# A two-layer streaming encoder step: query and key loads of the prompt attentions as 128-row transfers from one two-plane tensor

## The chip, the cores and the metric

One Trainium2 chip, one core of it. A core has five engines with their own instruction queues: TensorE (matmul; PE in the profile, its weight loads PEld), VectorE (DVE), ScalarE (ACT), GpSimd (POOL) and SyncE (SP), which here issues all the transfers; the transfers run on 16 DMA engines. Engines wait for each other by semaphores. The metric is the device time of one execution, in microseconds (us), as the median of several runs. TensorE's clock has two levels, 1.2 and 2.4 GHz; the profile gives the granted clock as a share of 2.4 GHz.

## The reference

The program is one step of a two-layer encoder, all in float32, on 1,024 frames of a new stream (the prompt) and on 16 new frames of each of 8 running streams (the samples), whose past is cached. Layer 0 has two attentions side by side: A, a sliding-window attention with 8 query and 2 key/value heads and a learned sink in each softmax, and B, a differential attention with 4 heads, each of two softmaxes. Layer 1 has C, a forgetting attention with 16 heads. A feed-forward block follows each. Cut to what matters here:

```python
# A (prompt): block-causal band of 3 chunks of 64 frames, 8 heads of 64
scores = q @ k.T * SCALE;  p = softmax([scores, sink])[..., :-1];  out = p @ v
# B (prompt and samples): 8 query/key halves of 64, 4 value heads of 128
p = softmax(where(chunk_mask, q2 @ k2.T * SCALE, NEG));  out = (p[0] - lam * p[1]) @ v
# C (prompt and samples): 16 heads of 64, c = cumsum(log_sigmoid(f)) along the frames
scores = q @ k.T * SCALE + c[query] - c[key];  p = softmax(where(causal, scores, NEG));  out = p @ v
```

## The kernel before, in words

The program runs in stages with a barrier of all engines between them: a projection of layer 0 (named abp in the profile), the prompt's window attention (pa), the samples' window attention (sa), a joint stage for the prompt's and the samples' differential attention (jb), output projection and feed-forward (abm, f), projection of layer 1 (c), the joint stage of the forgetting attention (jc), and again output projection and feed-forward (cm, f).

Queries and keys are kept in two parts. A float32 value is split into a high part that a fast matmul takes exactly and a low part, the rest. The projections write, for each of the prompt's queries (scaled) and keys, a row of 1,024 frames (4,096 bytes) into a tensor of high parts (`hi_ab`, `hi_c`) and one of low parts (`lo_ab`, `lo_c`) in the chip's memory. One head has 64 such rows. The scores of a query tile of 128 frames (`score`, L964 for pa and L1481 for jb and jc) are two matmuls for each piece of up to 512 keys, added up, and one that adds the mask:

- `q_hi` against `k_both`: `k_both` holds the key's 64 high rows on partitions 0 to 63 and its 64 low rows on 64 to 127; `q_hi` holds the query's high rows twice, so that the 128 products are high times high plus high times low.
- `q_lo` against `k_both` (pa, jb): the query's low rows twice. In jc instead `q_lo` against `k_hi` with 66 rows: 64 low rows against 64 high rows, and two rows of ones, which GpSimd writes once into `q_lo` (L1451 to L1454), against two rows of forget sums (`ck`).

So a head is loaded with six transfers of 64 rows (256 KB each), or with seven in jc (the seventh are the two rows of `ck`), by `load_qk` (L879 in pa, L1307 in jb and jc). The buffers hold two heads; a transfer group has one semaphore for each of the two, and the first `score` of a head waits for all of its transfers (L968, L1487); in pa it waits for the values and the sink of the head too (L969).

All transfers go out on SP's queue in the order written there. In pa: queries and keys, values, and sink of head 0, the same of head 1, and then for each head that is done the next but one. In jb and jc (L1381 to L1396): queries and keys of head 0, values, the key cache of the first sample stream (four transfers of 1 MB), the sample queries (four transfers with pieces of 256 bytes), then a wait for GpSimd's setup, small tables, the samples' new keys, queries and keys of head 1, its values. After that a loop over the units `u` (a head of the prompt and a stream of the samples each) issues the loads of the next units (L1397 to L1414).

TensorE works through an order that is written out by hand: for step `n` of a head `score(n+3)`, `turn(n+1)` (transposes of the probabilities), parts of the sample work, `attend` (probabilities times values). In the unit's step 5 it calls `score_new` (L1578 to L1581), which needs query blocks that VectorE copies (L1813) after it has turned the samples' new keys (L1828); `attend` (L1522) needs VectorE's scaling of the output before (L1803 or L1799). VectorE takes the maxima (L1768), turns the key cache 32x32-wise (L1822), and does the small sums.

Of the kernel before, what the change touches and what calls it, by code (L numbers as in the profile page):

```python
# [18 lines left out]
F32 = mybir.dt.float32  # L19
# [6 lines left out]
P = 128  # L26
D = 1024
# [757 lines left out]
def prompt_attention(nc, name, trips, q_rows, k_rows, v_cols, o_cols, hi, lo, y, o, dv, window=False,  # L785
# [40 lines left out]
    with Stage(nc, name) as st:  # L826
# [26 lines left out]
        n_qk_loads = 6 if ck is None else 7  # L853
# [20 lines left out]
        @block.sync  # L874
        def _(sp):
            if diff:
                sp.dma_start(lam[:], rows(b_lambda.rearrange("(a n) d -> a (n d)", a=1))).then_inc(lam_loaded, 16)

            def load_qk(i, e):  # L879
                k, q = bass.ds(k_rows(i, e), DH), bass.ds(q_rows(i, e), DH)  # L880
                upper, lower = slice(0, DH), slice(DH, P)
                sp.dma_start(k_both[upper, e].bitcast(F32), hi[k]).then_inc(qk_loaded[e], 16)
                sp.dma_start(q_hi[upper, e].bitcast(F32), hi[q]).then_inc(qk_loaded[e], 16)
                sp.dma_start(k_both[lower, e].bitcast(F32), lo[k]).then_inc(qk_loaded[e], 16)
                sp.dma_start(q_hi[lower, e].bitcast(F32), hi[q]).then_inc(qk_loaded[e], 16)
                sp.dma_start(q_lo[upper, e].bitcast(F32), lo[q]).then_inc(qk_loaded[e], 16)
                if ck is None:
                    sp.dma_start(q_lo[lower, e].bitcast(F32), lo[q]).then_inc(qk_loaded[e], 16)
                else:
                    sp.dma_start(k_hi[upper, e].bitcast(F32), hi[k]).then_inc(qk_loaded[e], 16)  # L890
                    sp.dma_start(k_hi[DH:DH + 2, e].bitcast(F32), ck[bass.ds(2 * i + e, 1)].rearrange(
                        "h a n -> (h a) n")).then_inc(qk_loaded[e], 16)

            def load(i, e):
                sp.dma_start(v[:, e], y[0:PROMPT, bass.ds(v_cols(i, e), dv)].rearrange(
                    "(t p) d -> p t d", p=P)).then_inc(loaded[e], 16)
                if sinks is not None:
                    s_i = sinks[0:1, bass.ds(2 * i + e, 1)]
                    sp.dma_start(sink[:, e:e + 1], rows(s_i)).then_inc(loaded[e], 16)

            def store(i, e):
                if diff and e == 0:
                    return
                sp.wait_ge(out_done, 2 + units * i + TILES_P * (e + 1))
                sp.dma_start(o[0:PROMPT, bass.ds(o_cols(i, e), dv)].rearrange("(t p) d -> p t d", p=P),
                             out[:, e]).then_inc(stored[e], 16)

            for q in stored:
                sp.nop().then_inc(q, 16)
            load_qk(0, 0)  # L910
            load(0, 0)
            load_qk(0, 1)
            load(0, 1)
            for i in range(trips - 1):
                for e in range(2):
                    sp.wait_ge(scores_done, units * i + TILES_P * (e + 1))
                    load_qk(i + 1, e)
                    sp.wait_ge(pv_done, 4 + units * i + TILES_P * (e + 1))
                    load(i + 1, e)
                    store(i, e)  # L920
            for e in range(2):
                store(trips - 1, e)
            sp.wait_ge(stored[1], 16 * (trips + 1))
            if not diff:
                sp.wait_ge(stored[0], 16 * (trips + 1))
# [223 lines left out]

def strided(ap, offset, *dims):  # L1150

    return bass.AP(ap.tensor, ap.offset + offset, [list(ap.ap[0])] + [list(d) for d in dims])


def joint_attention(nc, name, groups, hi, lo, k_first, v, v_cols, dv, q_sample, q_first, k_cache, v_cache, k_new, v_new,
# [79 lines left out]
    with Stage(nc, name) as st:  # L1235
        q_rows_lo = P if ck is None else DH + 2
        q_hi, k_both = st.sb("q_hi", [P, 2, PROMPT], F32R), st.sb("k_both", [P, 2, PROMPT], F32R)
        q_lo = st.sb("q_lo", [q_rows_lo, 2, PROMPT], F32R)
        k_hi = k_both if ck is None else st.sb("k_hi", [DH + 2, 2, PROMPT], F32R)
# [34 lines left out]
        n_qk_loads = 6 if ck is None else 7  # L1274
# [8 lines left out]
        else:  # L1283
            bias = st.sb("bias", [P, 2, bank + FRAMES])
            halves = st.sb("halves", [P, DH])
            later, select = st.sb("later", [P, FRAMES]), st.sb("select", [P, P])
# [19 lines left out]
        def _(sp):  # L1306
            def load_qk(h):  # L1307
# [3 lines left out]
                q, k = slice(q_first + h * DH, q_first + (h + 1) * DH), slice(k_first + h * DH, k_first + (h + 1) * DH)  # L1311
                upper, lower = slice(0, DH), slice(DH, P)
                sp.dma_start(k_both[upper, e].bitcast(F32), hi[k]).then_inc(qk_loaded[e], 16)
                sp.dma_start(q_hi[upper, e].bitcast(F32), hi[q]).then_inc(qk_loaded[e], 16)
                sp.dma_start(k_both[lower, e].bitcast(F32), lo[k]).then_inc(qk_loaded[e], 16)
                sp.dma_start(q_hi[lower, e].bitcast(F32), hi[q]).then_inc(qk_loaded[e], 16)
                sp.dma_start(q_lo[upper, e].bitcast(F32), lo[q]).then_inc(qk_loaded[e], 16)
                if ck is None:
                    sp.dma_start(q_lo[lower, e].bitcast(F32), lo[q]).then_inc(qk_loaded[e], 16)
                else:  # L1320
                    sp.dma_start(k_hi[upper, e].bitcast(F32), hi[k]).then_inc(qk_loaded[e], 16)
                    sp.dma_start(k_hi[DH:DH + 2, e].bitcast(F32), ck[h]).then_inc(qk_loaded[e], 16)
# [103 lines left out]
        def _(pool):  # L1426
# [22 lines left out]
            if ck is not None:  # L1449
                ones = probs[DH:DH + 2, 0]  # L1450
                pool.memset(ones, 1.0).then_inc(setup, 1)  # L1451
                for e in range(2):
                    pool.wait_ge(setup, 8 + e)
                    pool.tensor_copy(q_lo[DH:DH + 2, e], ones).then_inc(setup, 1)  # L1454
# [307 lines left out]
        def _(dve):  # L1762
# [126 lines left out]

            maximum(0)  # L1890
# [846 lines left out]
def build(nc, a, out):  # L2737
# [4 lines left out]
    hi_ab, lo_ab = (nc.dram_tensor(n, (13 * P, PROMPT), F32, kind="Internal").ap() for n in ("hi_ab", "lo_ab"))  # L2742
    hi_c, lo_c = (nc.dram_tensor(n, (2 * D, PROMPT), F32, kind="Internal").ap() for n in ("hi_c", "lo_c"))
# [47 lines left out]
    def v_rows_out(c, t, src):  # L2791
        if AB_PIECES[c][0] == VB:
            return [(b_v_out(t), src)]
        if t == TILES_P - 1:
# [3 lines left out]
    project_ab(nc, "abp", x0, gain(0, 0), a["w_ab_in"][0], a["rope_table"], hi_ab, lo_ab, qs_ab, v_ab, k_rows_out, v_rows_out, direct)  # L2798
    prompt_attention(nc, "pa", A_Q // 2, lambda i, e: (2 * i + e) * DH, lambda i, e: D + (i // 2) * DH,
                     lambda i, e: (i // 2) * DH, lambda i, e: (2 * i + e) * DH, hi_ab, lo_ab, v_ab, o_ab, DH,  # L2800
# [3 lines left out]
    joint_attention(nc, "jb", 1, hi_ab, lo_ab, D + P, v_ab, lambda h: P + h // 2 * P, P, qs_ab, 512,  # L2804
                    by_stream(a["cache_b_k"]), by_stream(a["cache_b_v"]), flat(out["b_k_sample"]), v_ab[samples, P:],
                    o_ab, A_Q * DH, row_odd=a["odd_heads"], b_lambda=a["b_lambda"][0])
    with Stage(nc, "m0") as st:
# [6 lines left out]
        project_c(nc, "c", ht_hi, ht_lo, a["w_c_in"][0], a["c_forget_bias"], a["cache_c_logf"][0], hi_c, lo_c, qs_c, v_c,  # L2814
# [3 lines left out]
    joint_attention(nc, "jc", 2, hi_c, lo_c, D, v_c, lambda h: h * DH, DH, qs_c, 0, by_stream(a["cache_c_k"]),  # L2818
# [40 lines left out]
```

## Time and profile before

| | |
|---|---|
| median of 3 runs | 3689.43 us (3681.23 to 3694.0) |
| profiled execution, first to last instruction (its own time is shown by this span alone) | 3685.0 us |
| TensorE busy | 3411.1 us, 93% of the span |
| VectorE, ScalarE, GpSimd busy | 43%, 30%, 7% |
| mean granted clock of TensorE | 0.964 |
| DMA engines, SP's queue | 490.36 MB, 42.8% of 16 engines' span |
| pa, jb, jc | 276 to 371, 414 to 716, 2084 to 2670 us of the span |

A time in the profile counts from the first instruction of the execution. "Busy" is the time in which an engine had an instruction in work; a busy TensorE runs at half its pace where its granted clock is 0.50. A row of the waits gives the instruction that was late, what it waited for, the total, the number of times and the longest. In a row of the timeline, what stands in brackets is the engine's idle time ahead of it and what ended it.

### The profile page before, as it was taken

What the parts mean: (1) busy time and instruction counts of PE and PEld (TensorE: products, weight loads), DVE (VectorE), ACT (ScalarE), POOL (GpSimd) and SP (SyncE); (2) the same over time, 40 slices, a digit from 0 to 9 for tenths busy, and PEclk for the clock granted to TensorE, in tenths of its full rate; (3) what the DMA queues carried; (4) which work ended last, traced back from release to release, by engine and by line L of the source; (5) the groups of instructions that cost most, each with busy time, mean ns of one, the idle gap of its engine ahead of it and who ended that gap; (6) DMA issues with size and microseconds to landing.
All of it is one profiled execution on the core that took longest, in us unless ns stands there. A gap on an engine that the chain in (4) does not pass through costs nothing. (4 is left out here: it accounts for less than half of the span.)

```text
span 3685.0 us, 63062 instructions
## 1 busy us (share of the span) xinstructions
PE 3411.1 (93%) x25000; PEld 2914.6 (79%) x25000; DVE 1597.5 (43%) x2910; ACT 1123.5 (30%) x2343; POOL 254.4 (7%) x340
## 2 busy tenths in 40 slices
PE   8998599788999999997899799999988999999997
PEld 7876466577999999996789666666567999999996
DVE  5417477463333333336231266666533333333334
ACT  4215255443112112113222245555433211211211
POOL 2310000032000000004000000000013000000003
PEclk9999799999999999998999899999989999999999
DMA  5438599443111111112554599999644111111102
GB/s 170 127 122 181 168 336 309 159 161 119 36 34 57 34 46 34 39 41 92 154 174 124 148 317 320 303 308 329 213 149 137 43 37 34 57 34 46 34 29 102
DMA packets 399665, 493.23 MB, mean 134 GB/s; under 512 B 69744, under 2 KB 251536, under 8 KB 399312
## 3 DMA queue, kind: packets, MB, share of 16 engines
q1 hardware_dynamic: 399456, 490.36, 42.8%
q8 instruction: 141, 2.31, 0.3%
q14 instruction: 68, 0.56, 0.1%
HBM read 407.10 MB, written 84.10 MB: 133 GB/s over the span
## 5 line engine op out<-in xcount | busy, mean ns | idle before, releaser
L2546 DVE TENSOR_TENSOR f_gated<-f_gated,f_up 128x384 f32<-128x384 f32 x132 | 73.1, 554 | 734.8 <-ACT f_gated L2476 734.8
L2570 DVE TENSOR_TENSOR f_y<-f_y,f_down 128x512 f32<-128x512 f32 x396 | 269.5, 686 | 229.6 <-PE f_down L2665 229.5
L2652 PE MATMUL f_gate<-m_ht_hi,f_w_hi 128*128 128x384 f32 x1056 | 355.0, 336 | 12.1 <-DVE f_w_lo L2597 12.1
L2652 PE MATMUL f_gate<-m_ht_lo,f_w_hi 128*128 128x384 f32 x1056 | 354.5, 336 | 0.0
L2652 PE MATMUL f_gate<-m_ht_hi,f_w_lo 128*128 128x384 f32 x1056 | 354.5, 336 | 0.0
L2652 PE MATMUL f_up<-m_ht_hi,f_w_lo 128*128 128x384 f32 x1056 | 352.7, 334 | 0.0
L2652 PE MATMUL f_up<-m_ht_hi,f_w_hi 128*128 128x384 f32 x1056 | 352.7, 334 | 0.0
L2652 PE MATMUL f_up<-m_ht_lo,f_w_hi 128*128 128x384 f32 x1056 | 352.7, 334 | 0.0
L2665 PE MATMUL f_down<-f_wo_hi,f_act_hi 128*128 128x512 f32 x792 | 312.6, 395 | 10.7 <-DVE f_y L2570 9.3
L2665 PE MATMUL f_down<-f_wo_lo,f_act_hi 128*128 128x512 f32 x792 | 309.2, 390 | 0.0
L2665 PE MATMUL f_down<-f_wo_hi,f_act_lo 128*128 128x512 f32 x792 | 309.1, 390 | 0.0
L2476 ACT ACTIVATE f_gated<-f_gate 128x384 f32<-128x384 f32 x132 | 65.0, 493 | 684.6 <-PE f_up L2652 684.3
L2652 PEld LDWEIGHTS f_gate<-m_ht_hi,f_w_hi 128*128 128x128 f32 x1056 | 199.6, 189 | 13.7 <-issue 12.9
L2652 PEld LDWEIGHTS f_gate<-m_ht_lo,f_w_hi 128*128 128x128 f32 x1056 | 199.6, 189 | 0.8
L2652 PEld LDWEIGHTS f_gate<-m_ht_hi,f_w_lo 128*128 128x128 f32 x1056 | 199.5, 189 | 0.0
L2652 PEld LDWEIGHTS f_up<-m_ht_hi,f_w_lo 128*128 128x128 f32 x1056 | 198.2, 188 | 0.0
L2652 PEld LDWEIGHTS f_up<-m_ht_hi,f_w_hi 128*128 128x128 f32 x1056 | 198.2, 188 | 0.0
L2652 PEld LDWEIGHTS f_up<-m_ht_lo,f_w_hi 128*128 128x128 f32 x1056 | 198.2, 188 | 0.0
L2665 PEld LDWEIGHTS f_down<-f_wo_hi,f_act_hi 128*128 128x128 f32 x792 | 149.2, 188 | 52.6 <-DVE f_y L2570 19.0
L1822 DVE STREAM_TRANSPOSE jc_kc<-jc_kc 128x512 f32<-128x512 f32 x256 | 180.9, 706 | 16.8 <-DMA jc_kc<-in_cache_c_k 2.7
L2665 PEld LDWEIGHTS f_down<-f_wo_hi,f_act_lo 128*128 128x128 f32 x792 | 148.9, 188 | 31.6
L2665 PEld LDWEIGHTS f_down<-f_wo_lo,f_act_hi 128*128 128x128 f32 x792 | 149.0, 188 | 29.6
(394 smaller groups left out, 6698.8 us busy)
## 6 DMA issues: line engine op xcount, KB each, us to landing
jc_kc<-in_cache_c_k SPq DMA_DIRECT2D x64, 1024.0 KB, 10.5
jc_vc<-in_cache_c_v SPq DMA_DIRECT2D x64, 1024.0 KB, 10.3
jb_kc<-in_cache_b_k SPq DMA_DIRECT2D x32, 1024.0 KB, 11.6
jb_vc<-in_cache_b_v SPq DMA_DIRECT2D x32, 1024.0 KB, 11.1
m_raw<-in_w_ffn_in SPq DMA_DIRECT2D x44, 512.0 KB
f_raw<-in_w_ffn_in SPq DMA_DIRECT2D x44, 512.0 KB
f_raw_o<-in_w_ffn_out SPq DMA_DIRECT2D x22, 1024.0 KB, 6.4
m_raw<-x SPq DMA_DIRECT2D x18, 512.0 KB, 4.1
```

The lines of the kernel that those rows point to most:

```text
L1822: dve.transpose(kc[:, u % 2, t, :], kc[:, u % 2, t + 1, :]).then_inc(kt_done, 1)
L2476: act.activation(silu[:, b], gate[:, q, 0:gw], ACT.Silu).then_inc(silu_done, 1)
L2546: dve.tensor_tensor(prod[:, b], silu[:, b], up[:, q, 0:gw], ALU.mult).then_inc(prod_done, 1)
L2570: dve.tensor_tensor(part, part, down[:, half, :], ALU.add).then_inc(added, 1)
L2652: last = pe.matmul(acc[:, q, 0:gw], a[:, s, k, u, :], b[:, k, token], start=(k == 0 and j == 0), stop=(k == KT - 1 and j == 2))
L2665: last = pe.matmul(down[:, half, :], a[:, s, t * P:(t + 1) * P], b[:, s, half * 512:(half + 1) * 512], start=(n == 0), stop=(n == 5))
```

## The change

The high and the low tensor of a layer become the two planes of one tensor (`planes_ab`, `planes_c`); the projections write into the planes as before. A helper `paired` describes a source that takes, for each of 64 rows, two rows in turn: with `second` true row r of plane 0 and row r of plane 1, otherwise the same row twice. A head's `k_both`, `q_hi` and (pa, jb) `q_lo` are loaded with one transfer of 128 rows each, whose partitions hold high and low rows (or the same row twice) in turn. pa and jb then have three transfers for a head.

In jc, `q_lo` and `k_hi` get 128 rows: the 64 low rows of the query and the 64 high rows of the key go to the even partitions, the two rows of `ck` to partitions 1 and 3 of `k_hi`. The odd partitions are set once: VectorE clears two score buffers, copies the zeros into `k_hi`, and adds to the zeros a column that GpSimd makes (1 on partitions 1 and 3, else 0) to fill `q_lo`. Before the first transfers into `q_lo` and `k_hi` SP waits for these three operations. jc has five transfers for a head, and its second score matmul has 128 rows for 66. The core of the diff (pa's `load_qk` is changed like that of jb, with `q_lo` always paired):

```diff
+def paired(planes, first, count, second):
+    top = planes[0, first:first + count]
+    step = planes[1].offset - planes[0].offset if second else 0
+    return bass.AP(top.tensor, top.offset, [list(top.ap[0]), [step, 2], list(top.ap[1])])
...
-        q_lo = st.sb("q_lo", [q_rows_lo, 2, PROMPT], F32R)
-        k_hi = k_both if ck is None else st.sb("k_hi", [DH + 2, 2, PROMPT], F32R)
+        q_lo = st.sb("q_lo", [P, 2, PROMPT], F32R)
+        k_hi = k_both if ck is None else st.sb("k_hi", [P, 2, PROMPT], F32R)
...
-        n_qk_loads = 6 if ck is None else 7
+        n_qk_loads = 3 if ck is None else 5
...
-                sp.dma_start(k_both[upper, e].bitcast(F32), hi[k]).then_inc(qk_loaded[e], 16)
-                sp.dma_start(q_hi[upper, e].bitcast(F32), hi[q]).then_inc(qk_loaded[e], 16)
-                sp.dma_start(k_both[lower, e].bitcast(F32), lo[k]).then_inc(qk_loaded[e], 16)
-                sp.dma_start(q_hi[lower, e].bitcast(F32), hi[q]).then_inc(qk_loaded[e], 16)
-                sp.dma_start(q_lo[upper, e].bitcast(F32), lo[q]).then_inc(qk_loaded[e], 16)
+                sp.dma_start(k_both[:, e].bitcast(F32), paired(planes, k, DH, True)).then_inc(qk_loaded[e], 16)
+                sp.dma_start(q_hi[:, e].bitcast(F32), paired(planes, q, DH, False)).then_inc(qk_loaded[e], 16)
                 if ck is None:
-                    sp.dma_start(q_lo[lower, e].bitcast(F32), lo[q]).then_inc(qk_loaded[e], 16)
-                else:
-                    sp.dma_start(k_hi[upper, e].bitcast(F32), hi[k]).then_inc(qk_loaded[e], 16)
-                    sp.dma_start(k_hi[DH:DH + 2, e].bitcast(F32), ck[h]).then_inc(qk_loaded[e], 16)
+                    sp.dma_start(q_lo[:, e].bitcast(F32), paired(planes[1:2], q, DH, False)).then_inc(qk_loaded[e], 16)
+                    return
+                if h == 0:
+                    sp.wait_ge(rows_set, 3)
+                sp.dma_start(q_lo[0:P:2, e].bitcast(F32), planes[1, q:q + DH]).then_inc(qk_loaded[e], 16)
+                sp.dma_start(k_hi[0:P:2, e].bitcast(F32), planes[0, k:k + DH]).then_inc(qk_loaded[e], 16)
+                sp.dma_start(k_hi[1:4:2, e].bitcast(F32), ck[h]).then_inc(qk_loaded[e], 16)
...
-                ones = probs[DH:DH + 2, 0]
-                pool.memset(ones, 1.0).then_inc(setup, 1)
-                for e in range(2):
-                    pool.wait_ge(setup, 8 + e)
-                    pool.tensor_copy(q_lo[DH:DH + 2, e], ones).then_inc(setup, 1)
+                pool.tensor_tensor(ones[:], ident[:, 1:2], ident[:, 3:4], ALU.add).then_inc(setup, 1)
+                pool.nop().then_inc(setup, 2)
...
+            if ck is not None:
+                empty = probs[:, 0:2]
+                dve.memset(empty, 0.0).then_inc(rows_set, 1)
+                dve.wait_ge(rows_set, 1)
+                dve.tensor_copy(k_hi[:], empty).then_inc(rows_set, 1)
+                dve.wait_ge(setup, 10)
+                dve.tensor_scalar(q_lo[:], empty, ones[:], None, ALU.add).then_inc(rows_set, 1)
             maximum(0)
...
-    hi_c, lo_c = (nc.dram_tensor(n, (2 * D, PROMPT), F32, kind="Internal").ap() for n in ("hi_c", "lo_c"))
+    planes_c = nc.dram_tensor("planes_c", (2, 2 * D, PROMPT), F32, kind="Internal").ap()
```

## Rows read from the trace of the kernel before

**Rows 1.** TensorE's waits, 270 to 2700 us: who waited for what, total, times, longest

```profile
PE jc_scores_a L1494 <- DMA jc_k_hi<-ck: 24.3, 2, 15.1
...
PE jb_scores_a L1494 <- DMA jb_q_lo<-lo_ab: 20.9, 2, 13.5
...
PE pa_scores L976 <- DMA pa_sink<-in_a_sinks: 15.7, 1, 15.7
```

**Rows 2.** Timeline, start of jb: start, us, engine, line, operation, count [idle before]

```profile
413.74 0.47 SPq L1313 DMA_DIRECT2D jb_k_both<-hi_ab  x1
...
423.45 0.77 PE L1494 MATMUL jb_scores_a<-jb_k_both,jb_q_hi 128*128 128x512 f32 x1 [13.47 <-DMA jb_q_lo<-lo_ab]
```

**Rows 3.** Stretches of jb's start: busy of PE, PEld, DVE, ACT, POOL; clock, DMA share, GB/s

```profile
417.00:419.00 2.00, 0.00 (x0) 0.00 (x0) 0.00 (x0) 0.00 (x0) 0.00 (x0) 0.50 0.99 215
...
428.00:433.00 5.00, 4.64 (x24) 4.05 (x23) 2.93 (x7) 3.51 (x10) 0.00 (x0) 0.76 1.04 383
```

**Rows 4.** Timeline, start of pa

```profile
276.26 0.52 SPq L882 DMA_DIRECT2D pa_k_both<-hi_ab  x1
...
287.38 0.44 PE L976 MATMUL pa_scores<-pa_k_both,pa_q_hi 128*128 128x128 f32 x1 [15.74 <-DMA pa_sink<-in_a_sinks]
```

**Rows 5.** Timeline of TensorE, second head of jb

```profile
449.55 0.80 PE L1494 MATMUL jb_scores_a<-jb_k_both,jb_q_hi 128*128 128x512 f32 x1 [7.41 <-DMA jb_q_lo<-lo_ab]
...
451.61 3.55 PE L1522 MATMUL jb_pv<-jb_probs_t,jb_vp 128*128 128x256 f32 x14
454.92 0.47 PE L1494 MATMUL jb_scores_b<-jb_k_both,jb_q_hi 128*128 128x512 f32 x1
```

**Rows 6.** Timeline of VectorE, second head of jb

```profile
447.69 0.32 DVE L1813 COPY jb_q_blocks<-jb_q_all 128x128 f32<-128x128 f32 x2
...
449.43 0.57 DVE L1803 TENSOR_SCALAR jb_out<-jb_pv,jb_inv 128x128 f32<-128x128 f32 x2
...
453.18 1.53 DVE L1822 STREAM_TRANSPOSE jb_kc<-jb_kc 128x512 f32<-128x512 f32 x2
```

**Rows 7.** One us of TensorE's wait in jb, columns as in rows 3

```profile
447.00:448.00 1.00, 0.00 (x0) 0.00 (x0) 0.95 (x5) 0.57 (x2) 0.00 (x0) 0.75 1.19 227
```

**Rows 8.** Timeline, start of jc

```profile
2084.06 0.47 SPq L1313 DMA_DIRECT2D jc_k_both<-hi_c  x1
...
2086.12 0.23 POOL L1445 COPY jc_halves<-jc_ident 64x64 f32<-64x64 f32 x1
...
2087.77 0.45 SPq L1322 DMA_DIRECT2D jc_k_hi<-ck  x1
...
2093.80 0.77 PE L1494 MATMUL jc_scores_a<-jc_k_both,jc_q_hi 128*128 128x512 f32 x1 [15.05 <-DMA jc_k_hi<-ck]
```

**Rows 9.** Groups of VectorE by shape: count, busy us, mean ns, idle before

```profile
L2555 DVE TENSOR_TENSOR f_wo_lo<-f_raw_o,f_wo_hi 128x2048 fp32r<-128x2048 f32 x22 | 50.3, 2286 | 0.4 <-ACT f_wo_hi L2485 0.4
...
L724 DVE TENSOR_SCALAR c_logf_s<-c_sum_s 128x2048 f32<-128x2048 f32 x1 | 1.2, 1222 | 0.0
```

**Rows 10.** Timeline of TensorE, second head of jc

```profile
2121.14 0.79 PE L1494 MATMUL jc_scores_a<-jc_k_both,jc_q_hi 128*128 128x512 f32 x1 [9.28 <-DMA jc_k_hi<-ck]
...
2123.84 2.40 PE L1522 MATMUL jc_pv<-jc_probs_t,jc_vp 128*64 128x256 f32 x14
```

**Rows 11.** One us in which sample queries (256-byte pieces) were loaded, columns as in rows 3

```profile
2107.00:2108.00 1.00, 0.00 (x0) 0.00 (x0) 1.00 (x4) 0.76 (x3) 0.00 (x0) 1.00 1.36 170
```

**Rows 12.** Groups of TensorE by shape: second score matmul with 66 and 128 rows

```profile
L1495 PE MATMUL jc_scores_b<-jc_k_hi,jc_q_lo 66*128 66x512 f32 x80 | 32.2, 403 | 0.0
...
L1495 PE MATMUL jb_scores_b<-jb_k_both,jb_q_lo 128*128 128x512 f32 x40 | 16.2, 404 | 0.0
```

**Rows 13.** Timeline of TensorE, key scores of a unit of jc

```profile
2236.05 6.21 PE L1556 MATMUL jc_s_ps<-jc_kc,jc_q_blocks 32*32 32x512 f32 x54 [1.86 <-issue]
```

**Rows 14.** Stretches of two units of jc, L1556 alone: busy PE, PEld, DVE, ACT; clock, DMA share, GB/s

```profile
2127.00:2134.00 7.00, 4.52 (x80) 1.39 (x80) 0.00 (x0) 1.09 (x2) 1.00 1.07 361
...
2232.00:2246.00 14.00, 9.82 (x80) 2.10 (x80) 0.00 (x0) 1.09 (x2) 0.65 0.89 186
```

## What the change is expected to do

> **What bounds the kernel now.** The list of what TensorE waited for comes first, since TensorE is busy 93% of the span: a change to loads can be worth only what TensorE, or whoever feeds it, waits for them. The reader is to see three entries there: the first score matmul of jc (24.3 us in two waits), of jb (20.9 in two) and of pa (15.7 in one), each ended by the last transfer of a load group [rows 1]. In time order these are five places: the starts of pa, jb and jc, and the second head of jb (7.41) and of jc (9.28) [rows 5, 10]. All later head loads are hidden: no other wait on them is in the list.
>
> Next come the stretches with their DMA rate. A load of six 64-row transfers is 6 x 64 x 4,096 bytes = 1.573 MB. At the start of jb nothing else is queued ahead; the first transfer is issued at 413.74 and the first score runs at 423.45, 9.71 us later [rows 2]. While those transfers move, the rate is 215 GB/s at a DMA share of 0.99; soon after, when only the 128-partition key-cache transfers move, it is 383 GB/s at 1.04 [rows 3]. So the engines are full in both, and the 64-row form moves about 0.57 of what the 128-row form does. 1.573 MB at 0.22 MB/us is 7.15 us; the other 2.56 of the 9.71 is issue to first byte and last byte to wake-up.
>
> **The change part by part.** *The transfer rate.* Sizes stay: three transfers of 128 rows are again 1.573 MB. No row shows a 128-row transfer whose source alternates between two planes. From above its rate is bounded by the 128-partition rows, 0.383 MB/us, from below by the slowest mixed stretch, 0.170, where 256-byte pieces move [rows 3, 11]. I take 0.383, the row whose destination has the same 128 partitions: 4.1 us instead of 7.15, so 3.05 us less for each load that is waited for, in whole. At the low end it is 9.25 us, 2.1 more. Fewer issues (0.6 us each) gain nothing of their own, since the queue is fuller than the engines can empty.
>
> *Start of pa.* The wait ends with the sink transfer, the eighth on the queue, behind the six and the values (0.26 MB) [rows 1, 4]. The first score runs at 287.38, 11.12 us after the first issue at 276.26. The six ahead shrink by 3.05; nothing else is late, so it goes to 284.4: **-3.0**. Bounds +2.1 and -3.05. VectorE paces the rest of pa, whose head loads stay hidden.
>
> *Start of jb.* Same arithmetic, and everything behind on SP's queue (values, key cache, sample queries, new keys, the second head) moves up with it, since it is bound by the engines: **-3.05**.
>
> *Second head of jb.* TensorE stops at 442.14 and gets the head at 449.55 [rows 5]. Shifted by the start and shortened by its own 3.05 the head is there at 443.45. Then the next wait is late: score_new needs the query blocks VectorE writes from 447.69, and attend needs the output scaling that ends at 450.00 [rows 6]; both are VectorE work in order behind the new keys, so they move only with the start, to 444.9 and 446.95. Attend, at 451.61 before, starts at 446.95, which is 1.6 beyond the start's 3.05. Beyond that the clock: TensorE idled from 442.14 and was granted half speed from the middle of 447 to 448 [rows 7]; the gap now ends at 443.45, 4.4 us after its own start (439.1). If the clock then stays at 2.4 GHz, the 3.3 us from 451.61 to 454.92 [rows 5] shrink to about 1.9 (the matmuls take half as long, some wait for copies stays): another 1.4. Next in line is VectorE's key turning, ended at 454.71 before and about 450.7 then, where TensorE would arrive; it costs nothing more. Together -1.6 - 1.4 = **-3.0**; bounds -1.6 and -3.05, or +2.1 with the low rate.
>
> *Start of jc.* Here work is added. VectorE clears two score buffers (128x2048), copies them to the high keys and adds a column of ones into the low queries, three passes in a row; SP waits for the third before it issues the low queries, high keys and forget sums of head 0 (the last of these went out at 2087.77 before [rows 8]), and behind SP's wait stand the values, the key cache, and all that follows. A pass is between 1.22 us (a 128x2048 scalar operation) and 2.29 (a two-input one of that size) [rows 9]; I take 1.22, the same kind of operation, and 3.9 with hops, from 2084.06 to 2088.0; the bad end is 6.9, to 2091. GpSimd's column of ones (its step before ends at 2086.35 [rows 8]) is then ready before the third pass. The two big transfers (1.05 MB) go out at once and are in by 2085.3 + 2.74 = 2088.0; the small ones start 1.25 after their issue, 2089.25, move 0.53 MB in 1.4 and wake TensorE 1.4 later: 2092.05 against 2093.80, **-1.7**; bounds -2 and +1.3. VectorE's passes lie before its first maximum, when it is idle. GpSimd loses three small operations, which nobody waited for.
>
> *Second head of jc.* It woke TensorE at 2121.14 after a wait of 9.28 [rows 10]. The start's 1.7 is passed on (the key cache comes behind the same queue) and the load is 3.05 shorter; VectorE's outputs for attend were done before it, so attend at 2123.84 moves by the whole: a further **-3.05**. The gap stays long enough that I expect half speed at its end, as now.
>
> *Matmuls with 128 rows for 66.* Low queries against high keys take 403 ns with 66 rows in jc and 404 with 128 in jb [rows 12]: nothing.
>
> *The sum.* -3.0 - 3.05 - 3.0 - 1.7 - 3.05 = -13.8 us. The profiled execution has a span of 3685.0, 4.4 under the median 3689.43 and inside the three runs (3681.2 to 3694.0), so 3671.2 on the span and **3675.6** on the median, -0.37%.
>
> **The rivals.** *No better rate.* The 64-row rate may be a limit the alternating form keeps (for instance if its engines meet at the same part of the memory). For it: share 0.99 at 215 GB/s says that the engines are held up, not why. Against it: the 128-partition rows. All four terms of 3 go; in jc the last small transfers then queue behind the big ones until 2092.5 and the passes are hidden: 3689, same.
>
> *High and low rows 8 MiB apart.* The trace before shows no transfer that alternates between distant rows; a high-key transfer of jc and a low-key one share the 215 to 230 GB/s of their stretch. In this kernel the mechanism would sit in the key transfer of jc, one of three, whose planes are 2,048 rows of 4 KB apart. If it ran at half today's rate, 0.52 MB would take 4.8 us instead of 2.4, against 2.0 gained on the queries: jc's two terms nearly vanish, and 3689.4 - 9 = 3680.4. The Trainium skill (DMA: Bandwidth & Descriptors, section Latency and other measured facts) states such a halving for rows that lie 4 or 8 MiB apart; no run here shows it, and it is stated for another copy, so I give it little.
>
> *Slower: the alternating source is spread worse.* If a source of 64 x 2 rows against a destination of 128 reaches fewer engines or goes in short pieces, each exposed load runs near 0.170 MB/us: five times +2.1, so 3700, and far more once the hidden loads no longer fit beside their heads. It decides from the point where the new rate is under 0.215. The Trainium skill (same page, section Why a DMA increments its semaphore by 16 and not by 1) has the engine count as the largest number up to 16 that divides both slowest dimensions; for 128 and 64 that is 16, and by it this case falls away; no row shows it.
>
> *The stall on issue moves.* In jc, TensorE waited for nothing the profile shows before a group of key scores at 2236.05 (1.86), and at a granted clock of 0.65 the 80 score matmuls of that unit were busy for 9.82 us, against 4.52 in an undisturbed one [rows 13, 14]: some 7 us lost. It lies among crowded DMA traffic, which shifts now: it may go (3668.5) or come a second time (3682.7).
>
> **How the numbers follow.** My sum 0.48; no better rate 0.2; 8 MiB 0.08; spread worse 0.1; stall gone 0.07, stall doubled 0.07. The bound for telling a change is 0.3%, 11.1 us, so 3678.4 and 3700.5. The sum lies 2.7 beyond it, so about three quarters of its weight is faster (0.37), with the stall gone 0.07 and a little of the 8 MiB case, 0.02: 0.46. Slower: half of the worse spread and a little of the rest, 0.07. The remaining 0.47 is within. Range 3666 to 3692: the stall's low end, and upwards the unchanged rate with the spread of the runs. The likeliest case alone is 3670 to 3681.
>
> **What would show it.** Right: the first score of jb about 6.6 us after its first issue, over 350 GB/s in between; jb's second wait under 5 us with the clock still full; jc's first score 8 us after its first issue with SP idle between two of its transfers for about 3; jc's second wait near 6. Wrong: 215 to 230 GB/s in those stretches again; VectorE's passes near 2.2 us each; new waits on loads in the list.

## The result, and the profile after

The changed kernel takes 3664.64 us (median of 4 runs, 3662.16 to 3666.87) against 3688.81 before (4 runs on the same chip): a ratio of 0.9936, 95% interval 0.9919 to 0.9953. That is 24 us, 0.64%, where 13.8 were forecast, and it lies under the forecast's range. The profiled executions show the same: spans of 3685.0 and 3661.3 us, 23.7 apart.

Where the time went is read first by stage. A stage begins with GpSimd's first write of its identity matrix; these are differences between those starts in the two profiles, in us. A unit of jc ends with TensorE's first bias-score matmul for that unit of samples; unit 0 begins with the stage:

| stage | before | after | measured | forecast |
|---|---|---|---|---|
| pa | 102.18 | 99.75 | -2.4 | -3.0 |
| jb | 318.40 | 312.19 | -6.2 | -6.05 |
| jc, unit 0 | 47.6 | 46.5 | -1.2 | -4.75 |
| jc, units 1 to 14 | 494.7 | 481.7 | -13.0 | 0 |
| all else in the span | 2722.1 | 2721.2 | -0.9 | 0 |

So pa and jb came out near the forecast, unit 0 of jc gained less, and more than half of the gain lies in a place to which the sum gave nothing. The places that the sum counted made 9.8 us of the 13.8 forecast; the other place made 13.0.

TensorE's waits over the same stretch as [rows 1] (who waited for what, total, times, longest):

```profile
PE jc_scores_a L1487 <- DMA jc_k_hi<-ck: 24.2, 2, 16.2
...
PE jb_scores_a L1487 <- DMA jb_q_lo<-planes_ab: 14.9, 2, 11.1
PE pa_scores L967 <- DMA pa_sink<-in_a_sinks: 13.5, 1, 13.5
```

The waits of pa and jb are shorter by 2.2 and 6.0 us. That of jc is not, and yet jc is 14 us shorter.

The starts of jb and pa (timeline; [rows 2, 4]), with the first score 7.36 us after the first issue in jb (9.71 before) and 8.85 in pa (11.12):

```profile
411.15 0.55 SPq L1309 DMA_DIRECT2D jb_k_both<-planes_ab  x1
...
418.51 0.76 PE L1487 MATMUL jb_scores_a<-jb_k_both,jb_q_hi 128*128 128x512 f32 x1 [11.12 <-DMA jb_q_lo<-planes_ab]
```

```profile
276.29 0.62 SPq L881 DMA_DIRECT2D pa_k_both<-planes_ab  x1
...
285.14 0.45 PE L967 MATMUL pa_scores<-pa_k_both,pa_q_hi 128*128 128x128 f32 x1 [13.46 <-DMA pa_sink<-in_a_sinks]
```

The rate while jb's first load moves (stretches, columns as in [rows 3]; the last two are DMA share and GB/s):

```profile
414.00:415.00 1.00, 0.00 (x0) 0.00 (x0) 0.00 (x0) 0.00 (x0) 0.00 (x0) 0.50 1.02 401
415.00:416.00 1.00, 0.00 (x0) 0.00 (x0) 0.00 (x0) 0.00 (x0) 0.00 (x0) 0.50 1.00 381
416.00:417.00 1.00, 0.00 (x0) 0.00 (x0) 0.00 (x0) 0.00 (x0) 0.00 (x0) 0.50 0.88 348
```

It was 215 at a share of 0.99; the value taken, 383, stands. But the first score came only 2.35 us earlier in the stage, not 3.05.

The second head of jb [rows 5], and its stretch [rows 7]:

```profile
440.55 0.50 PE L1487 MATMUL jb_scores_a<-jb_k_both,jb_q_hi 128*128 128x512 f32 x1 [3.82 <-DMA jb_q_lo<-planes_ab]
...
443.47 4.18 PE L1515 MATMUL jb_pv<-jb_probs_t,jb_vp 128*128 128x256 f32 x14 [1.25 <-DVE jb_out L1796]
447.30 0.77 PE L1487 MATMUL jb_scores_b<-jb_k_both,jb_q_hi 128*128 128x512 f32 x1
```

```profile
440.00:445.00 5.00, 3.08 (x40) 2.29 (x41) 4.68 (x12) 2.14 (x6) 0.00 (x0) 0.66 1.07 367
```

The wait is 3.82 us for 7.41. The scores behind it still run at full clock (0.50 us for 0.80), but the granted clock is 0.66 over the five us, and attend takes 4.18 us for 14 matmuls (3.55 before).

The start of jc (timeline; [rows 8]):

```profile
2075.69 1.76 DVE L1885 MEMSET jc_probs<- 128x2048 f32 x1 [4.70 <-PEq L69]
...
2077.49 1.23 DVE L1887 CAST jc_k_hi<-jc_probs 128x2048 fp32r<-128x2048 f32 x1
2077.57 1.20 POOL L1446 TENSOR_TENSOR jc_ones<-jc_ident 128x1 f32<-128x1 f32 x1
2078.81 2.08 DVE L1889 TENSOR_SCALAR jc_q_lo<-jc_probs,jc_ones 128x2048 fp32r<-128x2048 f32 x1
...
2080.91 0.47 SPq L1316 DMA_DIRECT2D jc_q_lo<-planes_c  x1
...
2086.08 0.76 PE L1487 MATMUL jc_scores_a<-jc_k_both,jc_q_hi 128*128 128x512 f32 x1 [16.20 <-DMA jc_k_hi<-ck]
```

The three passes take 1.76, 1.23 and 2.08 us. GpSimd's single column of ones, on which the third waits, takes 1.20 us beside the cast and ends 0.05 us after it, so that it delays next to nothing. SP's wait ends at 2080.9, and the first score comes 10.89 us after the first issue: later than before (9.74), where 8.0 was forecast. The second head makes up for this and 1.8 us more: its attend starts 37.98 us after the stage's first issue, 39.77 before [rows 10]:

```profile
2110.47 0.79 PE L1487 MATMUL jc_scores_a<-jc_k_both,jc_q_hi 128*128 128x512 f32 x1 [8.02 <-DMA jc_k_hi<-ck]
...
2113.17 2.18 PE L1515 MATMUL jc_pv<-jc_probs_t,jc_vp 128*64 128x256 f32 x13
```

**The units of jc.** These are stretches of one unit each, before (four units of 34, 34, 41 and 39 us) and after:

```profile
2132.00:2166.00 34.00, 33.10 (x499) 22.13 (x491) 25.06 (x54) 18.68 (x46) 0.00 (x0) 1.00 1.05 320
2166.00:2200.00 34.00, 33.09 (x500) 22.05 (x485) 23.39 (x52) 18.68 (x46) 0.00 (x0) 1.00 1.05 330
2200.00:2241.00 41.00, 36.10 (x489) 22.52 (x481) 23.19 (x52) 18.68 (x46) 0.00 (x0) 0.94 1.00 281
2241.00:2280.00 39.00, 38.09 (x507) 25.04 (x499) 23.20 (x52) 18.91 (x46) 0.00 (x0) 0.89 1.03 316
```

```profile
2122.00:2156.00 34.00, 33.09 (x499) 22.08 (x491) 25.15 (x54) 18.70 (x46) 0.00 (x0) 1.00 1.05 373
2156.00:2190.00 34.00, 33.09 (x500) 22.05 (x492) 23.19 (x52) 18.70 (x46) 0.00 (x0) 1.00 0.97 343
2190.00:2225.00 35.00, 33.39 (x489) 22.03 (x481) 23.18 (x52) 18.70 (x46) 0.00 (x0) 1.00 0.92 311
2225.00:2260.00 35.00, 34.09 (x511) 22.42 (x503) 23.19 (x52) 18.71 (x46) 0.00 (x0) 1.00 0.90 314
```

Read the last two columns. Before, the DMA engines are full (1.00 to 1.05) through all four units, at 281 to 330 GB/s. After, they move 373 in the first and on the mean have some room from the second on (0.97, 0.92, 0.90). The third and fourth unit are the long ones before, and the clock falls in them.

What stopped TensorE there (timeline before; the second gap is [rows 13]), and the DMA queues of the us 2224 to 2225 and 2232 to 2233 (packets, MB, share of 16 engines):

```profile
2224.08 0.42 PE L1578 MATMUL jc_turned<-jc_turned_new,jc_q_blocks 32*32 32x16 f32 x26
2226.63 0.21 PE L1578 MATMUL jc_turned<-jc_turned_new,jc_q_blocks 32*32 32x16 f32 x3 [2.13 <-issue]
```

```profile
q8 instruction: 1, 0.02, 6.6%
```

```profile
q8 instruction: 1, 0.02, 11.1%
```

A 16 KB packet of instructions begins in each of the two, 2.6 and 3.3 us before TensorE goes on. By the records they land at 2225.06 and 2234.54, 1.57 and 1.51 us before its next matmul. Beside a wait of up to 0.9 us for ScalarE's scores in each unit, units 1 to 14 have 44 gaps over 0.35 us in the two profiles and the twelve of the experiments, and all 44 end 1.24 to 1.71 us after such a packet has landed. So the releaser called issue is here the arrival of TensorE's own program. 40 of the 44 lie among the many small matmuls of the samples (`jc_turned`, `jc_s_ps`).

Each of these profiles has 55 such packets in the fourteen units, 770 in all. These are the five us before the packets of four gaps began, two before and two after:

```profile
2219.00:2224.00 5.00, 5.00 (x88) 4.11 (x86) 3.35 (x10) 2.73 (x8) 0.00 (x0) 1.00 1.04 386
2227.80:2232.80 5.00, 5.00 (x98) 4.08 (x99) 0.81 (x3) 1.83 (x6) 0.00 (x0) 1.00 1.11 211
```

```profile
2215.10:2220.10 5.00, 5.00 (x98) 3.92 (x98) 2.66 (x6) 2.00 (x7) 0.00 (x0) 1.00 1.08 326
2278.50:2283.50 5.00, 5.00 (x88) 4.23 (x86) 3.35 (x10) 2.84 (x8) 0.00 (x0) 1.00 1.06 363
```

The DMA engines were full ahead of all four, after too, where the mean of the unit is lower. Over all profiles, the share of the five us ahead was 1.00 or more for 497 of the 770 packets, and 43 of the 44 gaps come with these. So full engines go with a late packet, but most packets (454 of the 497) come in time all the same. The kernel before has 41 packets behind full engines and four gaps, the changed kernel 34 and two, the kernel with cut prompt loads (below) 24 and none.

Behind the second gap the clock falls (stretches before); the changed kernel's gaps, 0.51 and 1.00 us, bring no fall:

```profile
2230.00:2240.00 10.00, 8.13 (x106) 3.73 (x106) 3.97 (x7) 1.56 (x5) 0.00 (x0) 0.80 0.84 159
2240.00:2250.00 10.00, 10.00 (x78) 4.98 (x70) 3.42 (x8) 3.07 (x8) 0.00 (x0) 0.51 1.04 285
```

A clean unit takes 34.1 to 34.2 us. The 494.7 us are some 16 us over fourteen clean ones. The gaps are 5.3 of them; the granted clocks of the 20 us above (0.80 and 0.51) amount to some 14 us at half clock, which cost at most 7; the other 4 us have no place yet.

### The profile page after: what moved, and what is told of

Same layout as the page of the kernel before. It is cut to its first block and busy times, and to the rows that moved or that the text cites. A ratio compares the mean times of both kernels' runs of the same rounds, so it can differ in the third digit from the quotient of the medians.

```text
span 3661.3 us, 62984 instructions
## 1 busy us (share of the span) xinstructions
PE 3400.0 (93%) x25000; PEld 2909.1 (79%) x25000; DVE 1601.0 (44%) x2913; ACT 1123.9 (31%) x2343; POOL 254.6 (7%) x338
```

## The experiments

The theory: the spread loads empty the DMA queue of jc sooner, so that more instruction packets come in time. Each expectation is the text written before the run; "units" are the fourteen units 1 to 14, 494.7 us before, 481.7 after. They are read from one profiled execution of each kernel, while the time is the median of six to twelve.

**Only jc changed.** The loads of pa and jb are put back:

```diff
-        n_qk_loads = 3
+        n_qk_loads = 6
...
+                sp.dma_start(k_both[upper, e].bitcast(F32), hi[k]).then_inc(qk_loaded[e], 16)
```

> Only jc has the new loads and its new set-up; pa and jb keep six transfers of 64 rows to the upper and the lower half (out of the two planes). Theory A, a stall went: jc's gain of 14.15 us in the changed kernel is its two earlier heads, its later first head (together 0.6 to 3 us) and a stall of TensorE that fell away in unit 3 of the samples (gaps of 2.13 and 1.86 us that end on nothing but issue, then key scores that are busy 9.82 us instead of about 4.5). Then this kernel is 13 to 15 us faster than before, jc's span is 593.5 us instead of 607.6, and no gap of over 1.2 us on issue stands in jc. Rival, terms that add up: jc gains 0 to 5 us by its loads and the rest came from elsewhere; then 0 to 5 us faster. Rival, chance of timing: the stall goes whenever anything ahead of jc moves; here nothing ahead of jc moves, so it could stay, with 1 to 4 us faster.

3670.64 us, ratio 0.9946 (0.9928 to 0.9964): 17 us faster, where 13 to 15 were expected. jc takes 598.2 us (593.5 expected), units 486.7, in a profiled execution of 3676.59 us, 6 over the median. The gain is jc's, against the rival of 0 to 5 us; but gaps of up to 1.4 us stay, so "no gap over 1.2" was a miss (waits in units 1 to 14):

```profile
PE jc_turned L1589 <- issue: 2.6, 2, 1.4
PE jc_turned L1592 <- issue: 1.2, 1, 1.2
PE jc_pv L1533 <- issue: 0.4, 1, 0.4
```

**Only pa and jb changed.** jc gets its seven transfers, its 66 rows and its GpSimd set-up back.

> Only pa and jb have the new loads; jc keeps seven transfers with the extra rows behind the 64. Theory A: pa gains 2.4 us and jb 6.2 us, as in the changed kernel, and jc is as before (607.6 us), its stall in unit 3 with it (the two gaps on issue, key scores busy over 8 us): 8.6 us faster than before, 8 to 10. Rival, chance of timing: jc starts 8.6 us earlier, and a stall that hangs on such a shift goes: 8.6 + 12 = about 21 us faster with jc near 595 us.

3683.42 us, ratio 0.9989 (0.9976 to 1.0002): 4.3 us faster by the medians, not 8.6, and not clear of noise. In the profile (of an execution of 3676.83 us) jb gains 6.1 and pa 1.3; sa, between them, loses 2.9, its granted clock being 0.50 throughout, where it rose to 0.75 before. jc keeps its stall (two gaps of 2.1 us, units 491.5), though it begins 6.4 us earlier. That speaks against the chance of timing.

**Sample queries loaded later in the kernel before.**

```diff
-                    if (u + 1) % 4 == 0:
+                    if (u + 1) % 4 == 0 and diff:
                         load_q((u + 1) // 4)
...
                 load_values(u)
+                if u + 1 < U and (u + 1) % 4 == 0 and not diff:
+                    load_q((u + 1) // 4)
```

> The kernel before with one edit in jc: the four transfers of the samples' queries for the next four units (jc_q_all, 256-byte pieces) are issued behind that unit's values instead of ahead of the prompt's queries and keys. Theory A2, the stall comes of what stands in the DMA queues in unit 3, the small pieces of jc_q_all behind a backlog of cache keys: with them elsewhere the gaps of 2.13 and 1.86 us on issue and the long key scores go, and the kernel is 6 to 13 us faster with nothing else changed. Rival, the stall comes of the backlog of the whole stage, whichever transfer stands in it, or of the 64-row loads: the stall stays or moves to another unit, and the time is within 4 us of before.

3705.07 us, ratio 1.0045 (1.0031 to 1.0059): 17 us slower, units 509.8, seven waits on issue of 8.3 us in sum. Both numbers missed; the theory that the small pieces do it falls. The rival had the stall stay and the time within 4 us; the stall stayed, the time did not. The same bytes in another order cost 15 us more in the units.

**Sample queries cut, in both kernels.** The transfers for units 4, 8 and 12 bring 32 of 512 rows (a sixteenth; the expectations say a quarter by mistake):

```diff
+                cut = width if diff or g == 0 else Q
...
+                    sp.dma_start(q_all[Q * a:Q * a + Q, 0:cut // Q], q_sample[first:first + cut, streams].rearrange(
```

> The kernel before, but jc's four transfers of the samples' queries for units 4, 8 and 12 (jc_q_all) bring 32 of the 512 rows... of which each partition group then holds a quarter of what it should: 32 rows of 128, a quarter of the bytes and of the 256-byte pieces; the scores of those samples are computed from what the buffer held. Theory A2, the small pieces of jc_q_all hold up what TensorE has to fetch: its waits on issue in jc fall from 5.2 us to under 2.5, units 3 and 4 of jc (41.1 and 39.1 us before, 34.1 where nothing is late) come to 35 to 36, and the kernel is 8 to 13 us faster than before. Rival, the whole backlog does it (cache keys and values, 64-row loads): units 3 and 4 together still hold over 6 of their 12 us, and the kernel is at most 5 us faster.

> The changed kernel, but jc's transfers of the samples' queries for units 4, 8 and 12 bring a quarter of their rows, as in the same edit to the kernel before (the scores of those samples are computed from what the buffer held). By either theory little is left to go: units 3 to 5 of jc hold 35.3, 34.9 and 35.3 us in the changed kernel where 34.1 is clean, so 1 to 4 us faster than the changed kernel if jc_q_all is the cause of that rest, and within 1 us of it if it is not.

3687.37 us (1.0007, 0.9996 to 1.0018) and 3666.02 us (0.9939, 0.9923 to 0.9955): neither differs from its own kernel; units 494.1 and 481.0. In the kernel before the two gaps stay (2.1 and 1.1 us). The sample queries are not the cause, though the second gap of before lies among their transfers.

**Prompt loads cut in the kernel before.** For heads 2 to 15 of jc the six 64-row loads bring 64 of 1,024 frames (the expectation says 2,048 by mistake), a sixteenth of their bytes:

```diff
+                n = slice(0, PROMPT if ck is None or h < 2 else 64)
-                sp.dma_start(k_both[upper, e].bitcast(F32), hi[k]).then_inc(qk_loaded[e], 16)
+                sp.dma_start(k_both[upper, e, n].bitcast(F32), hi[k, n]).then_inc(qk_loaded[e], 16)
```

> The kernel before, but jc's six 64-row loads of queries and keys bring only 64 of 2048 columns for heads 2 to 15 (the scores of those heads are computed from what the buffers held). Theory A3, the 64-row loads (1.5 MB a head, at a lower rate than the others) are what kept the DMA queue full until unit 4: without them the backlog is gone by unit 2, jc's waits on issue fall under 2 us, units 3 and 4 come to 35 us, and the kernel is 12 to 16 us faster. Rival, jc_q_all alone does it wherever the backlog stands: units 3 and 4 still hold over 6 of their 12 us, at most 6 us faster.

3671.76 us, ratio 0.9959 (0.9944 to 0.9973), 15 us faster. Units take 479.1 us, the least of all runs, with no wait on issue in them. DMA share in units 1 to 3:

```profile
2135.00:2169.00 34.00, 33.10 (x499) 22.12 (x491) 25.45 (x54) 18.68 (x46) 0.00 (x0) 1.00 0.92 309
2169.00:2203.00 34.00, 33.09 (x492) 22.05 (x484) 23.21 (x52) 18.68 (x46) 0.00 (x0) 1.00 0.79 274
2203.00:2238.00 35.00, 34.10 (x516) 22.60 (x508) 23.29 (x53) 18.68 (x46) 0.00 (x0) 1.00 0.82 278
```

This run settles that the hidden loads bring the stall: with fifteen sixteenths of them gone, and nothing else, the stall is gone. It can't tell their form from their bytes. That the form is enough is shown by the runs with the same bytes in the new layout: only jc changed, and the next one.

**The new layout by transfers of 64 rows** to every second partition:

```diff
-                sp.dma_start(k_both[:, e].bitcast(F32), paired(planes, k, DH, True)).then_inc(qk_loaded[e], 16)
+                upper, lower = slice(0, P, 2), slice(1, P, 2)
+                sp.dma_start(k_both[upper, e].bitcast(F32), hi[k]).then_inc(qk_loaded[e], 16)
...
+                sp.dma_start(k_both[lower, e].bitcast(F32), lo[k]).then_inc(qk_loaded[e], 16)
```

> The changed kernel's layout, with high and low rows on alternating partitions, its planes and its set-up in jc, but each load as transfers of 64 rows to every second partition: six in pa and jb, seven in jc with the extra rows. Theory B1, a transfer's rate goes by the partitions that it spans: 64 rows spread over 128 partitions move as fast as 128, jb's first score stays 7.4 to 9 us after the first issue (three more issues of about 0.6 us), the bytes flow at over 300 GB/s from the second us on, and the kernel is within 6 us of the changed one. Theory B2, the rate goes by the rows of a transfer: about 215 GB/s as before, jb's first score 9.7 us after the first issue or later, jc's start later than in both kernels, and the time is within 6 us of before or above it.

3663.98 us, ratio 0.9939 (0.9924 to 0.9955): the time of the changed kernel, with six or seven transfers for a head. Units take 484.8 us. Three us of pa's first load:

```profile
276.00:277.00 1.00, 0.00 (x0) 0.00 (x0) 0.00 (x0) 0.00 (x0) 0.05 (x1) 0.50 1.01 311
277.00:278.00 1.00, 0.00 (x0) 0.00 (x0) 0.00 (x0) 0.00 (x0) 0.00 (x0) 0.50 0.93 377
278.00:279.00 1.00, 0.00 (x0) 0.00 (x0) 0.00 (x0) 0.00 (x0) 0.00 (x0) 0.50 0.75 164
```

The rate goes up and down; the mean of the first six us is 296 GB/s. So 64 rows spread over all partitions can flow well above the 215 of one half, and the time and the units follow the layout, not the 128 rows. At jb's start this does not show: the first score comes 10.0 us after the stage's start, as before the change (9.7) and not as after (7.4); its load flows at 152 to 356 GB/s with the engines not full (0.75 to 0.88). Why they idle there stays open, so the span of the partitions is the likely reason of the rate and not a proven one. The Trainium skill (SBUF — State Buffer, section Door 1: The DMA port swizzle) says that partitions 0 to 63 reach 8 of 16 ports, with 196 GB/s measured for 1 MiB, and all 128 reach 16. The 215 before and the 348 to 401 of the changed kernel agree.

**A shorter set-up in jc** (on the changed kernel):

```diff
-                dve.memset(empty, 0.0).then_inc(rows_set, 1)
-                dve.tensor_copy(k_hi[:], empty).then_inc(rows_set, 1)
-                dve.tensor_scalar(q_lo[:], empty, ones[:], None, ALU.add).then_inc(rows_set, 1)
+                for e in range(2):
+                    dve.memset(q_lo[:, e].bitcast(F32), 1.0).then_inc(rows_set, 1)
+                    dve.memset(k_hi[:, e].bitcast(F32), 0.0).then_inc(rows_set, 1)
```

> The changed kernel with a shorter set-up of jc's extra rows: VectorE writes ones and zeros straight into the first head's halves of jc_q_lo and jc_k_hi (two memsets of 128x2048), then into the second head's halves, in place of three passes over 128x2x2048 (1.76, 1.23 and 2.08 us) of which the third waits for GpSimd. SP's wait for the first head's rows should end about 1.8 to 2 us after VectorE's first memset begins instead of 5.2 us after it. Theory: the set-up was what made jc's first score come 10.89 us after the stage's first issue instead of the 7.4 us of jb; it comes at 7.5 to 8, and the kernel is 3 to 3.5 us faster than the changed one, 27 us faster than before. Rival: the samples' queries (9.87 us) or the transfers themselves set that first score, or what follows takes the gain back: within 1 us of the changed kernel, 24 us faster than before.

3661.13 us, ratio 0.9918 (0.9901 to 0.9935): the fastest kernel of the study, 26.6 us under before by the medians. The first score of jc comes 6.76 us after the first issue, where 7.5 to 8 was expected, 4.1 earlier than in the changed kernel, and unit 0 is 44.0 us for 46.5:

```profile
2079.89 0.91 DVE L1884 MEMSET jc_q_lo<- 128x1024 f32 x1 [4.50 <-PEq L69]
2080.97 0.91 DVE L1885 MEMSET jc_k_hi<- 128x1024 f32 x1 [0.16 <-issue]
```

Its interval overlaps the changed kernel's, so that the 2.5 us are shown in the profile and not by the times.

**Luck of the border?** TensorE's program in jc is to be shifted against its 16 KB blocks, first by 128 empty instructions:

```diff
+            if ck is not None:
+                for _ in range(128):
+                    pe.nop()
```

> The kernel before with 128 empty instructions ahead of TensorE's program in jc, which it passes while the first head's queries and keys are still on their way (9.7 us). They move the borders of the 16 KB blocks in which TensorE's instructions arrive, and nothing else: the data, its transfers and their order are as before. Theory A4: TensorE's waits on issue in jc end 1.2 to 1.7 us after a 16 KB instruction packet has landed, and packets come late wherever the DMA queue is full (share 1.00 to 1.05 in the units 1 to 4 of the kernel before), wherever the border falls: the gaps move to other lines, their sum in jc stays between 3 and 9 us, and the time stays within 10 us of before. Rival, luck of the border: the kernel before had an unlucky border in unit 3; moved, the gaps fall under 2 us and jc to about 595 us, 12 us faster than before.

> The changed kernel with the same 128 empty instructions ahead of TensorE's program in jc. Theory A4: the DMA queue is full for fewer units here (share 1.05 in unit 1, 0.97 in unit 2, 0.92 and below from unit 3 on), so packets come on time from unit 3 on, whatever the border: waits on issue in jc under 3 us in sum, jc between 590 and 598 us, within 5 us of the changed kernel. Rival, luck of the border: the changed kernel was lucky; moved, gaps of about 2 us come back with the clock's fall behind them, jc above 600 us and the time 8 to 15 us above the changed kernel.

3689.68 us (1.0002, 0.9992 to 1.0012) and 3665.49 us (0.9947, 0.9933 to 0.9961). The packets came beside the same matmuls as without them (the second of jc with matmul 151 in all four profiles), so nothing was shifted, and of the border they say nothing. They do show how far the stall scatters with the work unchanged: units 500.1 and 482.8 us. The second form used events, `pe.nop().then_inc(passed, 1)`:

> The kernel before with 128 semaphore events (each raises a semaphore that nobody waits for) ahead of TensorE's program in jc, while the first head's loads are under way. The 128 empty instructions tried before this left the packets of TensorE's instructions where they were (the packet that comes with matmul 151 of jc still comes with it), so they shifted nothing; events stand in the instruction stream. If a block border moves, the packets come beside other matmuls than 151, 350, 420 and 567. Theory A4: packets come late wherever the DMA queue is full, so waits on issue in jc stay between 3 and 14 us in sum, at other lines, and the time within 10 us of before. Rival, luck of the border: the waits fall under 2 us and the kernel is 10 to 14 us faster than before.

> The changed kernel with the same 128 events ahead of TensorE's program in jc. Theory A4: waits on issue in jc under 3.5 us in sum, jc between 590 and 599 us, the time within 5 us of the changed kernel. Rival, luck of the border: with another border gaps of about 2 us and the clock's fall come back, jc above 602 us and 8 to 15 us above the changed kernel.

3695.56 us (1.0020, 1.0006 to 1.0033) and 3670.00 us (0.9948, 0.9933 to 0.9964). The borders moved: the second packet comes with matmul 93 and 122. The events outlast the load (first score at 20.0 us), which makes unit 0 longer by 3.2 and 4.2 us. Waits in units 1 to 14, before:

```profile
PE jc_turned L1583 <- issue: 4.1, 2, 2.7
PE jc_s_ps L1616 <- issue: 3.8, 3, 1.7
PE jc_s_ps L1561 <- issue: 1.1, 1, 1.1
PE jc_scores_b L1500 <- issue: 0.6, 1, 0.6
```

and after:

```profile
PE jc_turned L1576 <- issue: 3.0, 2, 1.5
```

Units take 505.6 and 484.3 us. With these other borders the old loads still stall, elsewhere, and the new ones stall little, as expected (only jc of the changed kernel, 599.2 us, passed its bound of 599, with unit 0 longer): luck of the border falls as the explanation.

All profiles of full work together: with the old loads in jc the units take 491.5 to 509.8 us (before, pa and jb only, queries later, empty instructions, events), with the new layout 481.7 to 486.7 (after, jc only, 64 rows, shorter set-up, empty instructions, events). The two groups don't meet, and neither do the medians of their times (3683.42 us and more, 3670.64 and less).

## Why the prediction was wrong

- **The transfer rate** was right: 348 to 401 GB/s for the 383 taken. Its reason, left open by the rows, is probably the span of the partitions. With it fall the rivals of an unchanged or a worse rate, and that of rows 8 MiB apart: while jc's key transfer moves, the us 2077 to 2079 show 303 and 361 GB/s.
- **pa, jb's start and jb's second head** had the right mechanism: -2.4 and -6.2 for -3.0 and -6.05. Each start gained a little less than forecast (-2.3 and -2.35 for -3.0 and -3.05). Behind jb's second head the clock did not stay up (0.66), so attend to the next scores took 3.8 us where 1.9 was worked out. The wait on VectorE's outputs (1.25 us) came where it was named and ended 0.9 us earlier in the stage than worked out. The key turning, put at 450.7, would by the start's shift alone have ended at 451.7; TensorE did not wait for it. By those scores 5.0 us were gained (36.15 us after the stage's first issue, 41.18 before) and not 6.05; the other 1.2 us came later in jb, from what I can't say, so that the agreement of jb's total is partly luck.
- **The start of jc** was mis-sized. Three passes were taken at 1.22 us from one 128x2048 row, 3.9 us with hops; they took 5.07 in sum, and SP's wait ended 5.7 us after the first issue. From the issue of the low queries to the first score it then took 5.17 us, where 4.05 was worked out. Together +1.15 instead of -1.7, inside the bounds given (-2 to +1.3). The run with a shorter set-up returns 4.1 us at that place.
- **jc's second head**: -2.95 for -3.05; but some of it is given back before unit 0 ends, and -1.2 of the two terms is left.
- **The step that failed** is the sentence "All later head loads are hidden: no other wait on them is in the list." By it jc's units 1 to 14 got 0 in the sum; they measured -13.0. No matmul waits for those loads, but they keep the DMA engines full, and more of TensorE's instruction packets then come late. Of the 13.0, the gaps on issue give 3.6 (5.3 before, 1.7 after) and the half clock behind them up to 7; the rest is not placed. The stall was seen, among crowded traffic [rows 13, 14], and kept out of the sum as a rival that "may go (3668.5) or come a second time (3682.7)", 0.07 each. It should have been tied to the DMA share in jc's units (1.00 to 1.05 before), which the rate that the change was given must itself lower. The stall-gone case, at 3668.5, was 4 us from the result, but by luck: it has 13.8 and 7 where 9.8 and 13.0 were measured.

The Trainium skill (Runtime: NRT & Kernel Launch, section Instruction fetch mechanics) has instructions refilled in 16 KiB blocks over a DMA queue of the sequencer's own, at a cost that is mostly hidden. The trace agrees: the packets have 16 KB, and 726 of 770 came without a gap over 0.35 us. The other 44 held TensorE for up to 3.20 us, nearly all behind full engines.

What stays open: where a late packet loses its time (its own record takes 0.9 to 1.8 us, so the delay lies ahead of that, in a queue or in a late request), which of the packets behind full engines come late, and why the order of the same bytes (queries later) made it so much worse.

## What to carry to other kernels

A load that nobody waits for is not free where the DMA share is near 1: it can delay what else comes over the same engines, the program of TensorE among it. Here two such gaps of 4.0 us in sum were followed by some 14 us at half clock, which cost up to 7 more. Read the DMA share by unit of work, and in the few us ahead of a gap, as well as the list of waits, and look at the instruction packets beside each wait on issue. Lay a load out so that its destination spans all partitions, even if the rows must alternate, as the changed kernel does; and set up padding rows only as far as the first load needs them.

## What the runs showed of the hardware

- Where TensorE ran out of instructions, its next matmul followed the landing of a 16 KB instruction packet by 1.24 to 1.71 us (44 gaps, up to 3.20 us long). In the five us ahead of 43 of these packets the DMA share was 1.00 or more, as it was ahead of 454 that came in time.
- Transfers of 64 rows to every second partition flowed at 296 GB/s on the mean of six us at the start of pa (up to 377) and at 152 to 356 at the start of jb; those to one half at 215 in jb's start.
- GpSimd's sum of one column took 1.20 us beside VectorE's cast, and its 128x128 memset 1.16 us beside VectorE's scalar pass; the same memset took 0.20 us alone and 0.21 beside a VectorE memset.
- 128 empty instructions on TensorE left no trace in the packets; 128 events held its first score back to 20.0 us.
